# Modulation units placed anew in the weight ring, last-group sums taken product by product, zero products removed, and four waits moved, in a fused two-block transformer kernel

## The chip, the cores and the metric

The kernel runs as one program on one core of a Trainium2 chip, in float32. The metric is the device time of one execution in microseconds (us). Three executions of the kernel before took 1017.73, 1017.79 and 1018.97 us (median 1017.79). A fourth, recorded by the hardware profiler, took 1019.06 us; its trace spans 1017.3 us from the first to the last instruction, and all trace times below count from the start of that span.

## The reference, cut to what matters

A sequence of 256 tokens of width 1024 goes through two blocks. The first has two layers (`x + rms_norm(mixer(rms_norm(x)))`, four mixers of four heads each). The second, on which most of the change lies, has two layers whose inputs and residuals are modulated by a vector `c`:

```python
c_act = jax.nn.silu(c)
for i in range(DEPTH):                       # 2
    mods = jnp.split(c_act @ w_ada[i] + b_ada[i], 6, axis=-1)
    sh1, sc1, g1, sh2, sc2, g2 = [m[:, None, :] for m in mods]
    u = x * (1.0 + sc1) + sh1
    y = gla_mixer(...) if i == 0 else chunk_attention(...)
    x = layer_norm_2(DEEPNORM_ALPHA * x + (1.0 + g1) * y, ...)
    u = x * (1.0 + sc2) + sh2
    y = jnp.square(jax.nn.relu(u @ w1)) @ w2  # d_ff = 4096
    x = layer_norm_2(DEEPNORM_ALPHA * x + (1.0 + g2) * y, ...)
```

## The kernel before

**Names.** The 256 tokens are two tiles `t` of 128. `xt` is the residual stream, `xs` its normed form, `hT` the transposed, modulated input of the products (eight chunks of 128 features). `bank` is PSUM: eight banks of 128x512, `G[0..3]` and `A[0..3]`.

**The ring.** All large weights come as 180 units of 1 MB through six slots of `raw`. Unit `n` goes to slot `n % 6`. SyncE (SP) issues the transfers in order (L450), each after `used` of the same slot, that is, after the last reader of unit `n - 6`. A late reader of one unit therefore holds back that slot and all units after it in the queue. Most units are read by TensorE (PE). The modulation weights `w_ada` are units too, but VectorE (DVE) reads them: 24 units of the second layer's modulation go through `ada_unit_1`, by rows (`row_unit`, L905 and L909) or by columns (`column_unit`, L922). Their places in the ring are the table `ADA_1`, and the place in DVE's own program is where `ada_unit_1(ADA_1[a], a)` stands.

**GLA (N_GLA = unit 60 on).** Sixteen weight units and nine modulation units, `mma` six times, then `mmmm`, then `aaa`: eight of the nine are read during the mixer, the ninth (unit 84) in the first group of the feed-forward. `mixer_unit` and `mixer_sums` compute the projections with seven products in place of eight (a Strassen-like scheme whose sums DVE forms). Near the end, PE computes the last two gate projections into `G[2]` and `G[3]`, transposes the normed heads into `G[q]` for q = 0 to 3 (waiting for both gates before q = 2, L2413), and DVE multiplies by the gates (L1712). `out_product` and `out_sum`/`mixer_block` make the output projection.

**Feed-forward (`net` on PE, `groups` on DVE, `relu_groups` on ScalarE, ACT).** Sixteen groups of 256 hidden features. Group g has an up unit and a down unit; in layer 0 a modulation unit follows each of groups 1 to 15. For the first fifteen groups the down products also use seven products (`seven_products`, L2189) that accumulate over the groups in seven PSUM banks `SB`; before group 0 PE clears them by products on `zeros` (L2275). After the last of them DVE forms the four output blocks from the seven banks (`seven_sums`, L1529 to L1541) and adds the gated residual by column halves (`half_residual`, L1549 and L1552). The sixteenth group (`last_group`, L2241 and L2253) is computed plainly; its second half waits until DVE has read bank `A[2]` (`bank_free`), and its down products wait for `seven_ready`. Then come `modulation(1)` (L2132), `boundary` (L1326 to L1360) and the transposes of the next stage (L2141), copied to `hT` by ACT (L640).

**GpSimd (POOL)** forms the sums for three attention units in `quad_weights` (L523 to L528), the first of them as soon as the feed-forward's last unit is used. **The layer boundary in block one**: ACT squares the output halves (`y_square`, L611 to L616), then copies the transposed tile into `hT` (`layer_input`, L625), on which the first products of the next layer (L1921) wait.

The line that binds the ring to its readers:

```python
for s in range(SLOTS):
    sp.wait_ge(used[s], i)
    sp.dma_start(raw[:, s, :], units[i * SLOTS + s, :, :]).then_inc(landed[s], 16)
```

Of the kernel before, what the change touches and what calls it, by code (L numbers as in the profile page):

```python
# [14 lines left out]
P = 128  # L15
S = 256
# [60 lines left out]
AG = 9  # L77
NG = 16 + AG
N_GLA = DEPTH * U1
N_FF0 = N_GLA + NG  # L80
N_ATT = N_FF0 + 2 * GROUPS + 15
N_FF1 = N_ATT + 16

# [7 lines left out]
ADA_1 = [N_GLA + n for n in GA_AT] + [N_FF0 + 3 + 3 * g for g in range(SEVEN - 1)] + [N_FF0 + 2 + 3 * (SEVEN - 1)]  # L91
# [34 lines left out]
def build(nc, x, units, cols, small, post_g, consts, onehot, rel_bias, ccol, crow_in, colb_in, ada_rows,  # L126
          ln_rows, low_in, gk_in, att_line, v_row, out):
    with ExitStack() as ctx:  # L128
# [71 lines left out]
        def views(offset=0):  # L200
# [167 lines left out]
        tsum_ready, usum_ready = event("tsum_ready", 1), event("usum_ready", SEVEN - 1)  # L368
        last_up, bank_free = event("last_up", 1), event("bank_free", 1)
# [42 lines left out]
            ("ow_ready", 8), ("oi_ready", 2), ("op_ready", 7), ("ob_ready", 4)))  # L412

# [43 lines left out]
        def _(pool):  # L457
# [110 lines left out]
            n = N_FF1 + 2 * GROUPS - 1  # L568
# [6 lines left out]
        def _(act):  # L575
# [30 lines left out]
            def y_square(l, t):  # L606

                for i in range(2):
                    k = 2 * t + i
                    act.wait_ge(ob_ready.sem, ob_ready.at(l, k + 1))  # L610
                    act.activation(nl[:, 0:512], out_block[k], ACT.Square, accum_out=ssy[:, k:k + 1]).then_inc(osq_ready.sem, 1)  # L611
                    act.wait_ge(osq_ready.sem, osq_ready.at(l, k + 1))
                    if i == 0:
                        ch.do(act.activation(ybias[:, t:t + 1], ssy[:, k:k + 1], ACT.Identity, scale=1.0 / D, bias=eps_x[:]))
                ch.sync()
                act.activation(root[:, t:t + 1], ssy[:, k:k + 1], ACT.Sqrt, scale=1.0 / D,  # L616
                               bias=ybias[:, t:t + 1]).then_inc(sso_ready.sem, 1)

            def layer_input(l, t):

                for q in range(2 - t):
                    act.wait_ge(htp_ready.sem, htp_ready.at(l, 2 * t + q + 1))
                    for i in range(4):
                        c = 4 * q + i
                        act.activation(hT[:, c, t * P:(t + 1) * P], HB[t][q][:, i * P:(i + 1) * P], ACT.Copy,  # L625
                                       scale=pre[:, l, c:c + 1]).then_inc(ht_act.sem, 1)
# [20 lines left out]
            layer_input(0, 0)  # L647
            for l in range(DEPTH):

                layer_input(l, 1)  # L650
# [92 lines left out]
                y_square(l, 0)  # L743
                if l < DEPTH - 1:
                    x_square(l + 1, 0)
                else:
                    input_tile(0, 0, UB[0])
                y_square(l, 1)
                if l < DEPTH - 1:
                    layer_input(l + 1, 0)  # L750
                    x_square(l + 1, 1)
# [7 lines left out]
            def relu_groups(n0, per):  # L759

                step, lay = per // 3, n0 == N_FF1
                wait_used(act, 0, n0)
                act.activation(relu[:].rearrange("p c s -> p (c s)"), A[3][:], ACT.Relu).then_inc(relu_ready.sem, 1)
                for g in range(1, SEVEN):
# [4 lines left out]
                    wait_used(act, 0, n0 + 1 + step * (g - 1))  # L769
                    act.activation(prod[:, 4:7].rearrange("p i n -> p (i n)"), A[0][:, 0:3 * P], ACT.Copy).then_inc(prod_ready.sem, 1)  # L770
                n = n0 + step * SEVEN
# [3 lines left out]
                wait_used(act, 0, n)  # L775
# [56 lines left out]
            relu_groups(N_FF0, 9)  # L832
# [36 lines left out]
            relu_groups(N_FF1, 6)  # L869
# [9 lines left out]
        def _(dve):  # L879
# [644 lines left out]
            def seven_sums(last):  # L1524
# [3 lines left out]
                wait_used(dve, 0, last)  # L1528
                ch.do(dve.tensor_copy(c[0][0], p[0]))  # L1529
                ch.sync()  # L1530
                ch.do(dve.tensor_tensor(c[0][1], c[0][0], p[5], ALU.add))
                ch.do(dve.tensor_tensor(c[0][0], c[0][0], p[1], ALU.add))
                ch.sync(1)
                dve.sem_inc(bank_free.sem, 1)
                ch.do(dve.tensor_tensor(c[1][0], c[0][1], p[6], ALU.add))
                ch.do(dve.tensor_tensor(c[0][1], c[0][1], p[4], ALU.add))
                ch.sync(1)
                ch.do(dve.tensor_tensor(c[1][1], c[1][0], p[4], ALU.add))
                ch.do(dve.tensor_tensor(c[1][0], c[1][0], p[3], ALU.subtract))
                ch.sync(2)  # L1540
                dve.tensor_tensor(c[0][1], c[0][1], p[2], ALU.add).then_inc(seven_ready.sem, 1)  # L1541

            def half_residual(s, h):

                lay, g = s // 2, s % 2
                c = slice(h * 512, (h + 1) * 512)
                dve.wait_ge(seven_ready.sem, seven_ready.at(lay, 1))
                for t in range(NT):
                    ch.do(dve.tensor_tensor(ytmp[:, t, c], ytmp[:, t, c], gate_row[:, GATE_ROW[lay, g], c], ALU.mult))  # L1549
# [140 lines left out]
            for a in (4, 5):  # L1690
                ada_unit_1(ADA_1[a], a)
# [1041 lines left out]
```

## Time and profile before

| what | value |
|---|---|
| median of three executions | 1017.79 us (1017.73 to 1018.97) |
| the profiled execution: device time / span | 1019.06 us / 1017.3 us |
| PE matmul busy | 988.4 us, 97% |
| DVE busy | 773.6 us, 76% |
| ACT, POOL busy | 207.0 us (20%), 83.0 us (8%) |
| mean granted TensorE clock | 0.992 |
| DMA | 205.58 MB, mean 202 GB/s |

PE is busy for 988.4 of 1017.3 us, so what can be had without fewer products is at most the difference, 28.9 us, which includes the start and the tail. A row of the timeline reads: start in us, duration in us, engine, line, operation, tiles written and read, shapes, count of merged instructions, and in brackets how long the engine was idle before and what ended that. Each float32 product is recorded as two MATMUL instructions. The waits view sums such idle times by line and by what ended them.

### The profile page before, as it was taken

How to read it: one execution, taken by the hardware profiler on the slowest of the kernel's cores; microseconds unless marked ns; L12 is line 12 of the kernel's file. 1: busy time of each engine (PE TensorE's matmuls, PEld its weight loads, DVE VectorE, ACT ScalarE, POOL GpSimd, SP SyncE). 2: the span in 40 equal slices, each digit the busy share in tenths (PEclk: the TensorE clock that was granted, in tenths of full speed). 3: DMA queues.
4: the chain of work that ended last, by engine and by line, in shares of the span. 5: the costliest groups of instructions: out<-in, count | busy, mean ns of one | idle time of the engine just before them, and what ended most of it. 6: DMA issues, size and time to landing. Idle time of an engine off the chain costs nothing. (4 is left out here: it accounts for less than half of the span.)

```text
span 1017.3 us, 14206 instructions
## 1 busy us (share of the span) xinstructions
PE 988.4 (97%) x5326; PEld 722.5 (71%) x5328; DVE 773.6 (76%) x1761; ACT 207.0 (20%) x504; POOL 83.0 (8%) x91
## 2 busy tenths in 40 slices
PE   8999999999999999999899999989999999999996
PEld 4858755858766899747577777658996677777763
DVE  2697687696686887798799888985874677766677
ACT  4134314124322221201000000022223110000001
POOL 1100000000000000000002000062850000000020
PEclk9999999999999999999899999999999999999999
DMA  9955553855455746270879777824454345555511
GB/s 353 353 216 191 210 180 126 350 193 216 182 195 206 265 167 249 98 300 17 315 267 360 278 263 253 289 84 166 146 167 145 124 154 177 207 171 180 181 49 42
DMA packets 29916, 205.58 MB, mean 202 GB/s; under 512 B 3630, under 2 KB 3795, under 8 KB 6172
## 3 DMA queue, kind: packets, MB, share of 16 engines
q1 hardware_dynamic: 27116, 191.60, 51.6%
q0 software_dynamic: 2736, 13.11, 3.5%
q8 instruction: 42, 0.69, 0.3%
q14 instruction: 22, 0.18, 0.1%
HBM read 203.64 MB, written 1.05 MB: 201 GB/s over the span
## 5 line engine op out<-in xcount | busy, mean ns | idle before, releaser
L1859 PE MATMUL bank<-hT,raw 128*128 128x256 f32 x736 | 162.5, 380 | 0.0
L1859 PEld LDWEIGHTS bank<-hT,raw 128*128 128x128 f32 x736 | 138.7, 190 | 20.4 <-issue 1.7
L2189 PE MATMUL bank<-yT,arena 128*128 128x512 f32 x224 | 100.9, 593 | 0.4 <-DVE yT L1522 0.4
L2189 PE MATMUL bank<-raw,arena 128*128 128x512 f32 x180 | 88.7, 604 | 4.9 <-DMA raw<-units_dram 4.9
L2189 PEld LDWEIGHTS bank<-yT,arena 128*128 128x128 f32 x224 | 42.4, 190 | 54.5 <-issue 51.2
L922 DVE CUSTOM_DVE_ANT_0 raw<-raw,crow 128x1024 f32<-128x1024 f32 x64 | 75.4, 1220 | 1.1 <-DVEq L119 1.1
L2213 PEld LDWEIGHTS bank<-hT,raw 128*128 128x128 f32 x416 | 50.5, 192 | 12.4 <-issue 12.4
L768 ACT ACTIVATE arena<-bank 128x512 f32<-128x512 f32 x28 | 16.7, 597 | 196.9 <-PE bank L2213 196.9
L2213 PE MATMUL bank<-hT,raw 128*128 128x128 f32 x416 | 50.6, 275 | 0.0
L955 DVE SCALAR_TENSOR_TENSOR arena<-arena 128x256 f32<-128x256 f32 x120 | 48.4, 480 | 0.1
L2189 PEld LDWEIGHTS bank<-raw,arena 128*128 128x128 f32 x180 | 30.6, 194 | 22.0 <-issue 16.8
L1485 DVE TENSOR_TENSOR arena<-arena 128x256 f32<-128x256 f32 x28 | 13.4, 480 | 39.5 <-ACT arena L768 39.5
L2213 PE MATMUL bank<-arena 128*128 128x128 f32 x336 | 42.2, 275 | 0.0
L2213 PE MATMUL bank<-arena,gateT 128*128 128x128 f32 x336 | 42.2, 275 | 0.0
L2165 PE MATMUL bank<-hT,raw 128*128 128x128 f32 x256 | 37.2, 282 | 3.6 <-ACT hT L640 3.6
L909 DVE SCALAR_TENSOR_TENSOR ada<-raw,cact,ada 128x1024 f32<-128x1024 f32 x28 | 36.6, 1307 | 5.3 <-DMA raw<-units_dram 4.5
L2213 PEld LDWEIGHTS bank<-arena,gateT 128*128 128x128 f32 x336 | 39.9, 192 | 0.3
L2213 PEld LDWEIGHTS bank<-arena,raw 128*128 128x128 f32 x224 | 29.9, 194 | 13.9 <-issue 13.9
L2213 PEld LDWEIGHTS bank<-arena 128*128 128x128 f32 x336 | 39.7, 192 | 0.0
L770 ACT ACTIVATE arena<-bank 128x384 f32<-128x384 f32 x28 | 13.8, 491 | 114.1 <-PE bank L2213 114.1
L2165 PEld LDWEIGHTS bank<-hT,raw 128*128 128x128 f32 x256 | 32.7, 191 | 5.8 <-issue 5.2
L1939 PE MATMUL bank<-arena 128*128 128x512 f32 x72 | 32.4, 592 | 0.0
(462 smaller groups left out, 1817.6 us busy)
## 6 DMA issues: line engine op xcount, KB each, us to landing
raw<-units_dram SPq DMA_DIRECT2D x180, 1024.0 KB, 4.9
arena<-ln_rows_dram POOLq DMA_DIRECT2D x4, 1024.0 KB, 5.0
arena<-att_line_dram POOLq DMA_DIRECT2D x4, 512.0 KB, 5.5
arena<-small_dram POOLq DMA_DIRECT2D x2, 896.0 KB, 9.7
arena<-ada_rows_dram POOLq DMA_DIRECT2D x1, 1536.0 KB, 7.2
xt<-x_dram SPq DMA_DIRECT2D x2, 512.0 KB, 4.4
arena<-post_g_dram POOLq DMA_DIRECT2D x2, 512.0 KB, 8.7
kst<-consts_dram SPq DMA_DIRECT2D x1, 608.0 KB, 14.1
```

Of the source, the lines that this page charges most:

```text
L768: act.activation(prod[:, 0:4].rearrange("p i n -> p (i n)"), A[0][:], ACT.Copy).then_inc(prod_ready.sem, 1)
L770: act.activation(prod[:, 4:7].rearrange("p i n -> p (i n)"), A[0][:, 0:3 * P], ACT.Copy).then_inc(prod_ready.sem, 1)
L909: ins = dve.scalar_tensor_tensor(dst, w, cc, dst, ALU.mult, ALU.add)
L922: ins = dve.tensor_tensor_reduce(out=w, in0=w, in1=crow[:], scale=1.0, scalar=0.0, op0=ALU.mult, op1=ALU.add, accum_out=dst[:, c:c + 1])
L955: ins = dve.scalar_tensor_tensor(cacc[:, c, :], xg[:, c, j:j + S], w, cacc[:, c, :], ALU.mult, ALU.add)
L1485: ch.do(dve.tensor_tensor(csum[:, 0:5:4], prod[:, 0:1].to_broadcast([P, 2, P]), prod[:, 1:3], ALU.add))
L1859: mm = pe.matmul(b[:, c * S:(c + 1) * S], raw[:, s, k * 256 + c * P:k * 256 + (c + 1) * P], act_t[:, k, :], start=(k == 0), stop=(k == KC ...
L1939: mm = pe.matmul(OUT_BANKS[l][j][:], x[c] if isinstance(x, list) else x[:, c], y[c] if isinstance(y, list) else y[:, 512 * c:512 * (c + 1) ...
L2165: mm = pe.matmul(b[:, c * S + t * P:c * S + (t + 1) * P], raw[:, n % SLOTS, k * 256 + c * P:k * 256 + (c + 1) * P], hT[:, k, t * P:(t + 1) ...
L2189: return pe.matmul(SB[i][:], x, y, start=False, stop=stop)
L2213: mm = pe.matmul(A[0][:, i * P:(i + 1) * P], x(k), y(k), start=k == 0, stop=k == 3)
```

## The change

1. **Modulation units.** Two tables of letters set the ring: `GLA_ORDER` = `mma` four times, `mmaaaa`, `mmmmmmaaa` (eleven modulation units) and `FF_ORDER`, in which layer 0 has thirteen. On DVE unit a = 0 is read before the first stage's input, one more between the last mixer sums, three (a = 8, 9, 10) before the output sums, and groups 0 to 12 read one each; `coefficients(2)` and `(3)` follow group 12's.
2. **`seven_sums`.** The last group's seven products signal one by one (`last_product`), `5` is made before `4` and `6`, and DVE adds each bank when its product is done. The residual is now taken by tiles (`tile_residual`) and stands before the square that it followed.
3. **No zeros.** The first products carry `start=True`.
4. **Waits.** ACT at the layer boundary copies three chunks of `hT` before the last square; PE makes the first two products of mixer unit 0 before the decay rows and so before their wait; PE's transposes q = 2, 3 go to `A[2]`, `G[2]`, q = 3 waits for gate three only, and DVE waits for gate four; POOL starts `quad_weights` after both tiles are normed and its second one after `quad_tsum`.

```diff
-GW_AT = [w + w // 2 for w in range(12)] + [18 + w for w in range(4)]
-GA_AT = [3 * a + 2 for a in range(6)] + [22 + a for a in range(AG - 6)]
+GLA_ORDER = 4 * "mma" + "mmaaaa" + "mmmmmmaaa"
+FF_ORDER = ("u" + 13 * "uda" + "ud" + "dud", "u" + 14 * "ud" + "dud")
...
+        TURN_BANKS = (G[0], G[1], A[2], G[2])
...
-            wait_used(pool, 0, N_ATT - 1)
+            pool.wait_ge(xn_ready.sem, xn_ready.at(1, 2))
             quad_weights(0)
+            pool.wait_ge(quad_tsum, 1)
             quad_weights(1)
-            pool.wait_ge(xn_ready.sem, xn_ready.at(1, 2))
             quad_weights(2)
...
+                    y_square(l, 1, 0)
+                    layer_input(l + 1, 0, 0, 3)
+                    y_square(l, 1, 1)
+                    layer_input(l + 1, 0, 3, KC)
...
+                way = c[1][0]
+                dve.wait_ge(last_product.sem, last_product.at(lay, 1))
+                ch.do(dve.tensor_copy(way, p[0]))
+                ch.sync()
+                dve.wait_ge(last_product.sem, last_product.at(lay, 2))
+                ch.do(dve.tensor_tensor(c[0][0], way, p[1], ALU.add))
+                dve.wait_ge(last_product.sem, last_product.at(lay, 4))
+                dve.tensor_tensor(way, way, p[5], ALU.add).then_inc(bank_free.sem, 1)
+                dve.wait_ge(bank_free.sem, bank_free.at(lay, 1))
+                dve.wait_ge(last_product.sem, last_product.at(lay, 5))
+                ch.do(dve.tensor_tensor(c[0][1], way, p[4], ALU.add))
...
+                dve.tensor_tensor(c[1][0], way, p[3], ALU.subtract).then_inc(seven_ready.sem, 1)
...
                 for c in range(2):
+                    tile_residual(lay, c)
                     dve.wait_ge(relu_ready.sem, relu_ready.at(lay, 2 + c))
                     dve.tensor_tensor(hid[:, k, c], relu[:, c], relu[:, c], ALU.mult).then_inc(hid_ready.sem, 1)
-                    half_residual(s, c)
...
             for q in range(4):
+                if q == 2:
+                    out_weights(MIXER, 1, 1)
+                    out_weights(MIXER, 1, 2)
+                    dve.wait_ge(gate_ready, 4)
                 dve.wait_ge(ogp_ready, q + 1)
...
-            out_weights(MIXER, 1, 1)
-            out_weights(MIXER, 1, 2)
-            for a in (6, 7):
+            for a in (8, 9, 10):
                 ada_unit_1(ADA_1[a], a)
...
                 def product(i, x, y):
-                    return pe.matmul(SB[i][:], x, y, start=False, stop=stop)
+                    mm = pe.matmul(SB[i][:], x, y, start=g == 0, stop=stop)
+                    if stop and i != 3:
+                        mm.then_inc(last_product.sem, 1)
+                    return mm
...
-                    pe.matmul(b[:], zeros[:, 0:P], zeros[:], start=True, stop=False)
...
-            mixer_unit(0)
+            mixer_unit(0, between=decay_rows)
...
-                if q == 2:
-                    pe.wait_ge(gate_ready, 4)
+                if q == 3:
+                    pe.wait_ge(gate_ready, 3)
```

How the instructions stand on DVE between the gated heads and the output sums of the mixer, before (`raw,crow` and `raw,cact` mark modulation units, `arena<-raw` the weight sums of the output projection, `COPY arena<-bank` the first output sum):

```order
L1712 SCALAR_TENSOR_TENSOR yT<-bank,colb,gateT 128x256 x4
L1077 TENSOR_TENSOR arena<-yT 128x256
...
L1067 TENSOR_TENSOR arena<-raw,arena 128x1024
L1069 TENSOR_TENSOR arena<-arena,raw 128x1024
L1071 TENSOR_TENSOR arena<-raw 128x1024
L922 ISA raw,acc<-raw,crow 128x1024
L922 ISA acc 128x1
...
L1088 COPY arena<-bank 128x512
```

and now:

```order
L1087 TENSOR_TENSOR arena<-raw,arena 128x1024
L1089 TENSOR_TENSOR arena<-arena,raw 128x1024
L1091 TENSOR_TENSOR arena<-raw 128x1024
L1741 SCALAR_TENSOR_TENSOR yT<-bank,colb,gateT 128x256 x4
L1097 TENSOR_TENSOR arena<-yT 128x256
...
L925 TENSOR_SCALAR ada<-raw,cact 128x1024
L929 SCALAR_TENSOR_TENSOR ada<-raw,cact,ada 128x1024 x5
L1108 COPY arena<-bank 128x512
```

The three weight sums went ahead of the second gated pair, and three row units (six instructions) stand where two column units stood.

DVE at the end of layer 0's feed-forward, before:

```order
L1522 TENSOR_TENSOR gateT<-gateT,raw 128x512
L909 SCALAR_TENSOR_TENSOR ada<-raw,cact,ada 128x1024 x4
L1002 TENSOR_TENSOR arena<-acc,colb 128x16
...
L1529 COPY arena<-bank 128x512
...
L1541 TENSOR_TENSOR arena<-arena,bank 128x512
L1587 TENSOR_TENSOR arena<-arena 128x256
L1549 TENSOR_TENSOR arena<-arena 128x512 x2
L1552 SCALAR_TENSOR_TENSOR xt<-xt,arena 128x512 x2
```

and now:

```order
L1542 TENSOR_TENSOR gateT<-gateT,raw 128x512
L1551 COPY arena<-bank 128x512
L1554 TENSOR_TENSOR arena<-arena,bank 128x512
...
L1568 TENSOR_TENSOR arena<-arena,bank 128x512
L1576 TENSOR_TENSOR arena<-arena 128x512 x2
L1579 SCALAR_TENSOR_TENSOR xt<-xt,arena 128x512 x2
L1612 TENSOR_TENSOR arena<-arena 128x256
```

Two modulation units and the coefficients no longer stand ahead of the sums (they are in group 12 and before), and the first square (L1612, was L1587) follows its tile's residual.

## Rows read from the trace of the kernel before

**Rows 1.** Waits of PE: idle us in total, times, longest

```profile
PE bank L2189 <- DMA raw<-units_dram: 4.9, 1, 4.9
PE bank L2413 <- ACT gateT L816: 0.8, 1, 0.8
PE bank L2338 <- ACT arena L783: 0.5, 1, 0.5
```

**Rows 2.** Timeline of PE, feed-forward of layer 0, starts of groups 1 to 3

```profile
480.48 1.95 PE L2213 MATMUL bank<-hT,raw 128*128 128x128 f32 x16
...
489.11 3.78 PE L2189 MATMUL bank<-raw,arena 128*128 128x512 f32 x4 [4.88 <-DMA raw<-units_dram]
...
500.00 1.95 PE L2213 MATMUL bank<-hT,raw 128*128 128x128 f32 x16
...
512.27 1.95 PE L2213 MATMUL bank<-hT,raw 128*128 128x128 f32 x16
```

**Rows 3.** Timeline of DVE and of SP's queue at the same stall

```profile
482.76 4.00 DVE L909 SCALAR_TENSOR_TENSOR ada<-raw,cact,ada 128x1024 f32<-128x1024 f32 x3
...
484.22 1.96 SPq L450 DMA_DIRECT2D raw<-units_dram  x4
```

**Rows 4.** Windows: length, busy PE, PEld, DVE, ACT, POOL, PEclk, DMA share, GB/s

```profile
480.00:484.00 4.00, 4.00 (x34) 3.71 (x32) 3.93 (x6) 0.00 (x0) 0.00 (x0) 1.00 0.02 4
...
488.00:492.00 4.00, 2.89 (x4) 1.34 (x5) 2.59 (x4) 0.00 (x0) 0.00 (x0) 0.50 1.01 426
...
166.00:167.00 1.00, 1.00 (x3) 0.67 (x2) 1.00 (x1) 1.00 (x5) 0.00 (x0) 0.50 0.00 0
```

**Rows 5.** Timeline of all engines, layer boundary of block one

```profile
164.04 0.64 ACT L611 ACTIVATE arena<-gateT 128x512 f32<-128x512 f32 x1 [1.90 <-DVE gateT L1096]
...
165.00 2.16 ACT L625 ACTIVATE hT<-bank,pre 128x128 f32<-128x128 f32 x8
...
165.49 6.66 PE L1921 MATMUL bank<-raw,hT 128*128 128x352 f32 x16 [1.53 <-ACT hT L625]
...
169.65 0.75 DVE L1035 TENSOR_SCALAR xs<-xt,rst 128x1024 f32<-128x1024 f32 x1
...
171.99 1.04 PE L1909 MATMUL bank<-kst,xs 128*128 128x128 f32 x8
...
173.14 4.97 PE L1921 MATMUL bank<-raw,hT 128*128 128x352 f32 x16
```

**Rows 6.** Timeline of DVE and PE, starts of the two feed-forwards

```profile
468.37 0.69 DVE L1466 TENSOR_TENSOR arena<-hT,arena 128x512 f32<-128x512 f32 x1
...
469.79 1.95 PE L2213 MATMUL bank<-arena,gateT 128*128 128x128 f32 x16
...
814.80 0.69 DVE L1466 TENSOR_TENSOR arena<-hT,arena 128x512 f32<-128x512 f32 x1
...
815.79 1.24 PE L2275 MATMUL bank<-zeros 128*128 128x512 bf16 x5
```

**Rows 7.** Timeline of DVE and PE, end of the feed-forward of layer 0

```profile
648.76 5.31 DVE L909 SCALAR_TENSOR_TENSOR ada<-raw,cact,ada 128x1024 f32<-128x1024 f32 x4
...
653.28 3.62 PE L2241 MATMUL bank<-hT,raw 128*128 128x256 f32 x16
...
655.75 0.69 DVE L1529 COPY arena<-bank 128x512 f32<-128x512 f32 x1 [0.24 <-DVE arena L1016]
...
664.01 5.42 PE L2253 MATMUL bank<-raw,arena 128*128 128x512 f32 x12 [0.82 <-DVE arena L1587]
...
666.40 1.29 DVE L1326 TENSOR_TENSOR arena<-bank,arena 128x512 f32<-128x512 f32 x2
...
673.84 1.09 PE L2141 MATMUL bank<-kst,xs 128*128 128x128 f32 x8 [0.98 <-DVE xs L1360]
```

**Rows 8.** Line L1360, six tiles: ns min/median/max, first and last start us

```profile
L1360 DVE TENSOR_SCALAR xs<-xt,bag,rst x6: 811/814/1891, 453.2 to 808.2; 128x1024 f32<-128x1024 f32 x6
```

**Rows 9.** Timeline of DVE, first sum of the last boundary

```profile
1004.85 0.69 DVE L1387 CUSTOM_DVE_ANT_0 xt<-bank,xt 128x512 f32<-128x512 f32 x1 [0.21 <-DVEq L119]
```

More of the change, by code:

```diff
@@ L74, with places @@
 ARENA = 21104
-AG = 9
-NG = 16 + AG
+SEVEN = GROUPS - 1
+GLA_ORDER = 4 * "mma" + "mmaaaa" + "mmmmmmaaa"
+FF_ORDER = ("u" + 13 * "uda" + "ud" + "dud", "u" + 14 * "ud" + "dud")
 N_GLA = DEPTH * U1
-N_FF0 = N_GLA + NG
-N_ATT = N_FF0 + 2 * GROUPS + 15
+N_FF0 = N_GLA + len(GLA_ORDER)
+N_ATT = N_FF0 + len(FF_ORDER[0])
 N_FF1 = N_ATT + 16
-SEVEN = GROUPS - 1
-GW_AT = [w + w // 2 for w in range(12)] + [18 + w for w in range(4)]
-GA_AT = [3 * a + 2 for a in range(6)] + [22 + a for a in range(AG - 6)]
-ADA_1 = [N_GLA + n for n in GA_AT] + [N_FF0 + 3 + 3 * g for g in range(SEVEN - 1)] + [N_FF0 + 2 + 3 * (SEVEN - 1)]
+def places(order, what, at=0):
+    return [at + n for n, c in enumerate(order) if c == what]
+UP, DOWN = ([places(FF_ORDER[lay], c, (N_FF0, N_FF1)[lay]) for lay in range(2)] for c in "ud")
+assert all(len(n) == GROUPS for n in UP + DOWN)
+GW_AT, GA_AT = places(GLA_ORDER, "m"), places(GLA_ORDER, "a")
+AG = len(GA_AT)
+ADA_1 = [N_GLA + n for n in GA_AT] + places(FF_ORDER[0], "a", N_FF0)
+assert len(GW_AT) == 16 and len(ADA_1) == 24
 RE = 2 * DEPTH
@@ L628, in root_of, with layer_input @@
+            def layer_input(l, t, c0, c1):
+                for c in range(c0, c1):
+                    q, i = c // 4, c % 4
+                    if i == 0:
+                        act.wait_ge(htp_ready.sem, htp_ready.at(l, 2 * t + q + 1))
+                    act.activation(hT[:, c, t * P:(t + 1) * P], HB[t][q][:, i * P:(i + 1) * P], ACT.Copy,
+                                   scale=pre[:, l, c:c + 1]).then_inc(ht_act.sem, 1)
             def root_of(s, t):
@@ L831, in _ @@
             stage_tiles(1)
-            relu_groups(N_FF0, 9)
+            relu_groups(0)
             stage_tiles(2)
@@ L1550, in half_residual @@
-                for t in range(NT):
+                for c in h:
+                    ch.do(dve.tensor_tensor(ytmp[:, t, c], ytmp[:, t, c], gate_row[:, GATE_ROW[lay, 1], c], ALU.mult))
+                for c in h:
                     ch.sync(1)
@@ L1553, in half_residual, with groups @@
                 ch.sync()
-            def groups(s, n0, per):
-                step, lay = per // 3, s // 2
+            def groups(s):
+                lay = s // 2
+                up, down = UP[lay], DOWN[lay]
                 token_sums(s, tsum, tsum_ready.sem)
@@ L1562, in groups @@
                     up_half_sums(s, g + 1)
-                    weight_sums(n0 + 2 + step * g)
+                    weight_sums(down[g])
                     up_rest_sums(s, g + 1)
@@ L1757, in _ @@
             normed(0, 1)
-            up_sums(N_FF0 + 1, 1)
+            up_sums(UP[0][1], 1)
             stage_tiles(1)
-            groups(1, N_FF0, 9)
-            boundary(1, y_told(1, 3) + y_used(N_ATT - 1))
+            groups(1)
+            boundary(1, y_told(1, 3) + y_used(DOWN[0][-1]))
             stage_tiles(2)
@@ L2305, in mixer_unit @@
                 product(0, lambda k: w[:, k, 0:P], lambda k: hT[:, k, 0:P])
+                if between is not None:
+                    between()
                 product(1, lambda k: w[:, 4 + k, 0:P], lambda k: hT[:, 4 + k, 0:P])
@@ L2687, in lay_out @@
         f2 = [w2[256 * g:256 * (g + 1)].reshape(2, P, D).transpose(1, 0, 2).reshape(P, UNIT) for g in range(GROUPS)]
-        units.append(f1[0])
-        for g in range(1, SEVEN):
-            units += [f1[g], f2[g - 1]]
-            if l == 0:
-                units.append(ada1[AG + g - 1])
-        units.append(f2[SEVEN - 1])
-        if l == 0:
-            units.append(ada1[AG + SEVEN - 1])
-        units += [f1[SEVEN], f2[SEVEN]]
+        rest = {"u": iter(f1), "d": iter(f2), "a": iter(ada1[AG:])}
+        units += [next(rest[c]) for c in FF_ORDER[l]]
         if l == 0:
```

179 lines of the change are left out of this document (79 added, 100 removed).

## The prediction, made before the changed kernel was run

> **What bounds the kernel now.** The table above says it first: PE is busy for 97% of the span, at almost full clock. So the question is never "which engine is shorter" but "where does PE stand still, where does it run at half clock, and which of its products go". I read four views in that order. The waits view of PE gives the stops by cause: the longest single one is 4.9 us for a weight unit, and two short ones of 0.8 and 0.5 us end on ACT [rows 1]. The timeline round the long stop shows what it really costs [rows 2], and the queue's own timeline what released it [rows 3]. The windows tell a full DMA system from an empty one, and half clock from full [rows 4]. Last come the timelines at the places where one stage hands over to the next [rows 5 to 8]; the reader is to look there for the time in brackets and its releaser.
>
> **The ring, 7.2 us.** A group takes 500.00 to 512.27, that is 12.27 us; the group from 480.48 took until 500.00, 19.52 us [rows 2]. The difference, 7.25 us, is the 4.88 us stop plus some 2.4 us of slow products behind it: four of them took 3.78 us [rows 2], at a granted clock of 0.50, the 1.2 GHz level [rows 4]. Why did the unit come late? In the four microseconds before the stop the DMA share was 0.02 [rows 4]: nothing was being fetched. SP issued at 484.22, within DVE's modulation products of group 0, and the unit landed 4.9 us later, when PE went on [rows 2, 3]. Counting units: the down unit of group 1 is unit 90, slot 0, whose predecessor is unit 84, the ninth modulation unit, which DVE reads only in group 0. It held up slot 0 and all behind it. In the new order N_FF0 is 87, that down unit is 92, and its predecessor 86 is read by DVE before the mixer's output sums, a stage earlier. Every other predecessor of group 0's and 1's units (81 to 85) is read earlier still. In the groups each slot is released in the group before its unit is needed, as before, and the group at 500.00 shows no stop. I take the whole 7.25 us. Bounds: 0 if another unit takes its place, 7.25 if none does.
>
> DVE pays for this. Before the output sums it now does three row units, six instructions, where two column units stood; a row instruction takes about 1.3 us (5.31 for four [rows 7]), so 2.4 to 2.9 us more. But it no longer stands still for the last two output units: they come in slots 82 % 6 and 83 % 6, whose predecessors are modulation units 76 and 77, read before the gates are computed; before, the last one's was the last gate's weight unit. Two more units stand in idle time of DVE in the mixer. Behind the three units the output sums are queued, and PE's feed-forward behind these. I cost it at nothing; without the cover it would be 2.9 us.
>
> **Two waits in the mixer, 1.2 us.** The decay rows' wait on ACT (0.5) goes behind two products that need nothing, and the wait for gate four (0.8) leaves PE [rows 1]; DVE takes it, but reaches it only after three weight sums. PE stays the bound up to the feed-forward, so I take 0.5 + 0.8, less 0.1. Bounds 0 and 1.3.
>
> **The layer boundary, 1.2 us.** PE waited 1.53 us for ACT's first copy at 165.00; ACT had idled 1.90 us before the last square at 164.04 [rows 5]. Now three copies (0.27 each, 2.16 for eight) use that idle time. PE starts almost 1.5 us sooner and ACT's next five copies follow in time. But PE then meets the second tile: its normed form was ready at 169.65 + 0.75 = 170.40, and this chain hangs on the last square, which the three copies push back by about 0.3 (0 to 0.8). So PE can begin the second transposes at 170.8 instead of 171.99 [rows 5]: a gain of 1.2, not 1.5. The rest becomes a new wait of up to 1.8 us on DVE's `xs`. Whether the first tile runs at half clock, as it did (6.66 us against 4.97 for the same products, clock 0.50 [rows 4, 5]), no longer matters, since PE would wait anyway. Bounds 0.7 and 1.5.
>
> **No zeros, 2.3 us.** Seven products on zeros per feed-forward; five are recorded in 1.24 us, the last one's tail lying over the next product, so about 0.22 each, 1.5 per feed-forward [rows 6]. In layer 1 the token sums end at 814.80 + 0.69 = 815.49, about when PE gets there: all 1.5 is gained. In layer 0 they end at 469.06 and PE went on at 469.79 [rows 6], so the first six give about 0.65 and then a wait for DVE; with the seventh, 0.85. Bounds 1.5 and 3.
>
> **The end of the first feed-forward, 2.6 us.** Before, DVE did 5.31 us of modulation and the coefficients, and began the seven sums at 655.75, 2.5 us after PE's last product of seven (653.28) [rows 7]. Now it starts at about 649 and follows: PE makes a 128x512 product of two instructions in some 0.9 us (5.42 for twelve), DVE needs 0.69 or less per sum (0.65 per operation in a pair of 1.29) [rows 7], and after PE's last at 653.28 only three sums remain, so `seven_ready` comes near 655.1. A tile's residual is four of these operations, 2.6 us: first square near 658.2, second near 661.3. PE meanwhile runs without a stop: the last group's up products 7.2 us (3.62 for half of them [rows 7]), the last group's down products (sixteen instructions) and the modulation rows (eight) another 10.3 at 0.43 each, the tail of the twelve taken off: from 653.28 to 670.8. The stops of 0.82 and 0.98 us [rows 7] and the shorter ones between go. Does DVE have the tile by then? It began the boundary at 666.40 [rows 7]; now it waits for PE's second output block (four products of 0.86 after 660.5), near 663.9, and is there for the next step about 2.9 us earlier, so the tile, ready for PE at 673.84, is ready at 670.9 even at the old durations. PE begins the transposes at 670.8 to 670.9 in place of 673.84: 3.0 us. Against it: group 12 now carries both a row unit and the coefficients (654.07 to 655.75, 1.7 us [rows 7]), of which DVE's idle time in a group takes the larger part. Between 0 and 1.7 I take 0.5 us of PE waiting, since two places in each group let DVE wait for ACT. Net 2.6 us, bounds 1 and 3.4.
>
> The slowest L1360 took 1891 ns against 811 [rows 8]; it is this boundary's first tile, while POOL was forming `quad_weights`. The Trainium skill (SBUF — State Buffer, Who interferes with whom) says that the two engines share a port pair as an exclusive lock, the loser blocked for the whole instruction; the trace agrees in size. By that rule the moved POOL wait gives DVE 1.1 us back on this chain. In my sum it is worth at most 0.1, because PE's own work until 670.8 then covers it. POOL's second and third unit now come after the token sums, but PE needs them only in the second and third quarter of the first heads, behind three projections: no cost.
>
> **The end of the kernel, 0.4 us.** DVE began the last boundary at 1004.85, just free of the residual (0.21 us idle for its own work) [rows 9]. Freed of it sooner, it is bound by PE's output blocks, whose last ends no earlier than before, counted from PE's last product of seven. Between nothing and one more operation of 0.7 us on each side, I take 0.4, bounds 0 and 1.4.
>
> **The sum.** 7.25 + 1.2 + 1.2 + 2.3 + 2.6 + 0.4 = 14.95 us. The profiled execution took 1019.06 us (span 1017.3), so 1004.1 and a span of 1002.3. That execution lies 1.3 us above the median of the three others, 1017.79; against the median it is 1002.8. I give **1003.0**.
>
> **The rivals.**
> - *The clock falls in a new place.* Before the half-clock stretch at 166 PE had stopped for 1.53 us [rows 4, 5]; my new wait at about 169 to 170.8 is as long, and stands before products that nothing hides. The price is what the same products lost there, 6.66 - 4.97 = 1.7 us: 1004.7. Chance 0.2. The Trainium skill (TensorE: Matmul & The Clock Gate, What's actually happening) says that activity, not demand, releases the throttle; by that rule any new stop is suspect, and so would be the zero products' removal in layer 0, where PE now idles 0.65 us.
> - *The stop moves rather than goes.* DVE is now the only reader ahead of units 90 to 92, and any one read late stops PE in group 0 or 1. For it: slots are few, and DVE is nearly full in groups 1 to 4. Against: by the count above these three are released before the output sums. A stop of the old size costs 7.25: 1010.2. Chance 0.1. That the change does not do what it says (the unit late for bandwidth, not for its slot) is the same case; the DMA share of 0.02 ahead of the stop speaks against it [rows 4], though it was 1.01 once the four issues had gone.
> - *The sums do not pay.* DVE meets PE's products too late, or group 12 falls further behind, and 2.6 becomes 0: 1005.6. Chance 0.08.
> - *Slower.* Unit 86 is issued only when PE starts on the output projection's second half-input, and DVE's output sums, `xs`, the first feed-forward and thus PE are queued behind its reading. From the time at which it is just hidden, each us that it lands later costs one. By my count it is just in time; to be slower than 1017.8 it would have to land over 15 us later than the 4.9 us seen at the stop. Price 15 and more: 1018 or above, chance 0.02.
>
> **How the numbers follow.** Forecast 0.60, clock 0.20, moved stop 0.10, sums 0.08, slower 0.02. A measurement of this kernel tells about 0.2% from no change, 2 us. The forecast's own bounds (mixer and zeros a little less, boundary a little more) are about 999.8 to 1005; with the clock and the sums the range reaches 1007.5, and leaves out most of the moved stop and the slower case. All cases but the last are faster by more than 2 us: faster 0.97, same 0.01, slower 0.02.
>
> **What would show it.** In the new profile: no wait of PE on a DMA in the feed-forward, and groups 0 to 3 all of 12.3 us; no row of `zeros` after the start, and a wait of PE on DVE's token sums in layer 0 only; a wait on `xs` of up to 1.8 us at the layer boundary with none on the first copy; the seven sums starting before PE's last product; no PE wait on POOL or on `asum`. The forecast is wrong if PE busy plus PE's stops does not fall by about 14 us, and wrong in its largest term if a DMA stop stands anywhere between the mixer and group 3.

## The result, and the profile after

The changed kernel took 1004.47 us in the median of four runs (1003.33 to 1005.85), the kernel before 1018.38 us beside it (1017.73 to 1019.66). The ratio is 0.9862, with a 95% interval of 0.9845 to 0.9880: 1.4% faster. The forecast was 1003.0 us, its range 999.8 to 1007.5. The profiled execution took 1004.16 us (span 1002.4), 14.90 us less than the profiled one of before; the forecast's sum was 14.95. The medians lie 13.91 us apart.

PE's waits after the change (idle us in total, times, longest); the three rows of [rows 1] are gone, and the two longest that remain hang on DVE and ACT:

```profile
PE bank L2192 <- ACT hT L657: 3.6, 8, 1.3
PE bank L1936 <- DVE xs L1055: 2.7, 3, 1.7
PE bank L1928 <- POOL zeros L474: 1.3, 1, 1.3
PE bank L1948 <- ACT hT L642: 1.1, 1, 1.1
PE bank L2243 <- DVE arena L1486: 0.5, 1, 0.5
PE bank L2216 <- DVE yT L1542: 0.4, 1, 0.4
```

The starts of groups 1 to 3, on PE's timeline, answer to [rows 2], and the windows over the same stretch (busy PE, PEld, DVE, ACT, POOL, then PEclk, DMA share, GB/s) to [rows 4]:

```profile
477.56 1.95 PE L2243 MATMUL bank<-hT,raw 128*128 128x128 f32 x16
...
489.83 1.95 PE L2243 MATMUL bank<-hT,raw 128*128 128x128 f32 x16
...
502.10 1.95 PE L2243 MATMUL bank<-hT,raw 128*128 128x128 f32 x16
```

```profile
480.00:484.00 4.00, 4.00 (x27) 3.04 (x26) 3.58 (x7) 0.60 (x1) 0.00 (x0) 1.00 0.75 260
484.00:488.00 4.00, 4.00 (x22) 2.68 (x21) 3.02 (x8) 0.49 (x1) 0.00 (x0) 1.00 0.74 258
488.00:492.00 4.00, 4.00 (x25) 2.93 (x24) 3.93 (x9) 0.00 (x0) 0.00 (x0) 1.00 0.65 240
```

Group 1 takes 12.27 us where it took 19.52. The DMA share is even, where it had been 0.02 and then 1.01, and the clock stays at 1.00.

The layer boundary, which answers to [rows 5]: no wait for the first copy, three copies, the square, five copies, and the new wait on `xs`:

```profile
163.93 0.89 ACT L642 ACTIVATE hT<-bank,pre 128x128 f32<-128x128 f32 x3 [1.42 <-PE bank L1936]
...
164.44 4.97 PE L1948 MATMUL bank<-raw,hT 128*128 128x352 f32 x16
164.70 0.64 ACT L626 ACTIVATE arena<-gateT 128x512 f32<-128x512 f32 x1
...
165.66 1.38 ACT L642 ACTIVATE hT<-bank,pre 128x128 f32<-128x128 f32 x5
...
171.11 1.09 PE L1936 MATMUL bank<-kst,xs 128*128 128x128 f32 x8 [1.70 <-DVE xs L1055]
```

The end of the first feed-forward, which answers to [rows 7]: DVE takes up the sums while PE still makes the last group's products, waits for some of them, and has the first tile's `xs` before PE needs it:

```profile
639.00 0.68 DVE L1551 COPY arena<-bank 128x512 f32<-128x512 f32 x1
...
641.26 0.69 DVE L1556 TENSOR_TENSOR arena<-arena,bank 128x512 f32<-128x512 f32 x1 [0.85 <-PE bank L2216]
...
645.02 0.69 DVE L1568 TENSOR_TENSOR arena<-arena,bank 128x512 f32<-128x512 f32 x1
...
653.38 0.69 DVE L1346 TENSOR_TENSOR arena<-bank,arena 128x512 f32<-128x512 f32 x1 [1.73 <-PE bank L2283]
...
659.07 0.81 DVE L1380 TENSOR_SCALAR xs<-xt,bag,rst 128x1024 f32<-128x1024 f32 x1
...
660.84 1.04 PE L2168 MATMUL bank<-kst,xs 128*128 128x128 f32 x8
```

Laid over one another, the two PE timelines give the place of every microsecond (before to after, start of the same products):

| stretch | forecast | measured |
|---|---|---|
| start of the kernel (another DVE and ACT wait there) | 0 | -0.38 |
| layer boundary | 1.2 | 1.20 |
| two waits in the mixer (0.34 and 0.97) | 1.2 | 1.31 |
| zeros, layer 0 and layer 1 | 0.85 + 1.5 | 0.78 + 1.43 |
| the ring, group 1 | 7.25 | 7.25 |
| lost again in the groups (0.40 of it in group 12) | -0.5 | -0.52 |
| end of the first feed-forward, gross | 3.0 | 3.35 |
| end of the kernel | 0.4 | 0.41 |

With 0.07 us of small shifts this is 14.90 us. Every term that was forecast came out within 0.35 us, and yet the experiments show that two of them had another cause than the one given.

### The profile page after: what moved, and what is told of

The parts are those of the page before. It is cut to its first block, busy times and chain, and to the rows that moved or that the text cites. A ratio compares the mean times of both kernels' runs of the same rounds, so it can differ in the third digit from the quotient of the medians.

```text
span 1002.4 us, 14184 instructions
## 1 busy us (share of the span) xinstructions
PE 982.2 (98%) x5314; PEld 719.6 (72%) x5314; DVE 771.3 (77%) x1761; ACT 206.7 (21%) x504; POOL 82.8 (8%) x91
## 4 chain that ended last, share of the span: by engine, by line
PE 50%; DVE 3%; issue 0%; ACT 0%; DVEq 0%; ACTq 0%
PE bank L2216 17%; PE bank L2243 16%; PE bank L2500 6%; PE bank L2519 2%; PE bank L2192 2%; PE bank L2271 1%; PE bank L2283 1%; PE bank L1896 1%; PE bank L2485 1%; PE bank L1886 1%; PE bank L1913 1%; PE bank L2539 0%; PE bank L2159 0%; PE bank L2530 0%; PE bank L2528 0%
```

## The experiments

"Longer" and "shorter" below are read like the table, by laying PE's timeline over that of the changed kernel's profile. That resolves about 0.05 us, where the medians of the runs resolve 1 to 2 us.

**e1: the old ring with all the rest of the change.**

```diff
-GLA_ORDER = 4 * "mma" + "mmaaaa" + "mmmmmmaaa"
-FF_ORDER = ("u" + 13 * "uda" + "ud" + "dud", "u" + 14 * "ud" + "dud")
+GLA_ORDER = 6 * "mma" + "mmmmaaa"
+FF_ORDER = ("u" + 14 * "uda" + "daud", "u" + 14 * "ud" + "dud")
```

and DVE's reads at their old places (unit 84 in group 0, the last unit and the coefficients behind the groups).

> The changed kernel with the old order of units in the ring and the old places of the modulation reads on DVE; all else of the change stays. Slot theory: unit 84 is again read only in group 0, so PE stops for about 4.9 us on a weight unit ahead of group 1's products and runs some of them at clock 0.50; the group from about 477.6 takes 19.5 us instead of 12.3, and the run about 7.25 us longer than the changed kernel, near 1011.7. The coefficients are again behind the groups, so the end of the first feed-forward gives back up to 2 us more: up to 1013.5. Rival (what helped was that PE's or DVE's other edits loosened the fetching): no stop of over 1 us in the feed-forward, about 1004.5.

Measured: 1018.62 us, ratio to before 0.9989 (0.9975 to 1.0003). The whole gain is gone, 13.84 us in the timelines. PE's waits and timeline of this kernel:

```profile
PE bank L2217 <- DMA raw<-units_dram: 4.8, 1, 4.8
...
PE bank L2284 <- DVE arena L1615: 2.9, 1, 2.9
...
PE bank L2272 <- DVE arena L1556: 0.9, 1, 0.9
PE bank L1967 <- DVE yT L1742: 0.8, 1, 0.8
```

```profile
487.15 3.78 PE L2217 MATMUL bank<-raw,arena 128*128 128x512 f32 x4 [4.80 <-DMA raw<-units_dram]
...
656.15 3.72 PE L2272 MATMUL bank<-hT,raw 128*128 128x256 f32 x16 [0.91 <-DVE arena L1556]
...
662.78 8.64 PE L2284 MATMUL bank<-raw,arena 128*128 128x512 f32 x16 [2.91 <-DVE arena L1615]
```

The slot theory stands: the stop and the slow products are back, 19.61 us for the group instead of 12.27. What was missed is the rest. In the mixer DVE again stands 5.31 us for an output unit ahead of the gate turns (4.98 in the kernel before), and PE, which no longer waits for gate four and so comes sooner, waits 0.83 us for the first of these turns: most of the 0.97 us won at that wait is lost again. And at the end of the feed-forward 5.85 us are lost where I allowed 2: with the last unit and the coefficients behind the groups DVE begins the sums at 654.08, and PE runs into `bank_free` (0.91), into the last squares, which now stand behind a whole tile's residual (2.91), and into half clock (8.64 us for sixteen products that took 7.03). The new order of sums and residual is good only while DVE is early: over the same stretch the kernel before, whose DVE is as late but whose sums and residual are the old ones, takes 3.35 us more than the changed kernel, and so 2.5 us less than this one; 1.6 us of the 2.5 are the half clock.

**e2: the kernel before with one read moved.**

```diff
-                        if g == 0:
-                            ada_unit_1(ADA_1[8], 8)
...
-            for a in (6, 7):
+            for a in (6, 7, 8):
```

> The kernel before with one line moved: DVE reads the ninth modulation unit (unit 84) ahead of the output sums instead of in group 0; the order of the ring stays. Slot theory: the stop of 4.9 us and the slow products behind it go, 7.25 us less, about 1011; DVE's extra 2.6 us ahead of the output sums may show as up to 1 us of waiting. Rival (the place in the ring is what counts, since unit 84 would land too late to be read early, or its successors would): a stop of 2 us or more stands at the output sums or in group 0, and the gain is under 4 us, 1014 or more.

Measured: 1015.31 us, ratio to before 0.9958 (0.9942 to 0.9975). No stop on a DMA stands in the feed-forward, and from the first group to the last products of seven this kernel gains 7.16 us on the one before. The profile as a whole gains only 5.41, because 0.85 us are lost at the start, 0.78 by DVE's extra unit (PE waits 0.94 us on `xs` ahead of the feed-forward) and 1.63 by half clock at 344 (the last section), while 1.54 are won at the layer boundary (see e4). So the reading of one unit was the whole stall; its place in the ring was not.

```profile
464.38 1.09 PE L2139 MATMUL bank<-kst,xs 128*128 128x128 f32 x8 [0.94 <-DVE xs L1360]
```

**e3: the old sums and residual in the changed kernel.** `seven_sums` waits for all seven products and then works in pairs; the residual goes by column halves behind each square.

```diff
-                dve.wait_ge(last_product.sem, last_product.at(lay, 1))
+                wait_used(dve, 0, last)
...
-                    tile_residual(lay, c)
                     dve.wait_ge(relu_ready.sem, relu_ready.at(lay, 2 + c))
                     dve.tensor_tensor(hid[:, k, c], relu[:, c], relu[:, c], ALU.mult).then_inc(hid_ready.sem, 1)
+                    half_residual(s, c)
```

> The changed kernel with the seven sums begun only after all seven products of the last group (in two pairs, and with the residual in halves by column), as before the change; ring, zeros and waits stay changed. If following the products one by one is what pays: PE's stops of 0.8 and 1 us at the end of the first feed-forward return, and the kernel is 1.0 to 1.5 us longer there and 0.4 us longer at its end, about 1006. Rival (the gain came from moving the last modulation unit and the coefficients away, and PE's work covers the sums anyway): under 0.3 us at the first feed-forward, 1004.8.

Measured: 1005.16 us, 0.9854 (0.9837 to 0.9870). At the end of the first feed-forward nothing is lost: PE starts the boundary's transposes at 660.73, as in the changed kernel (660.84), and without a wait, though DVE begins the sums 4.7 us later:

```profile
643.73 0.69 DVE L1550 COPY arena<-bank 128x512 f32<-128x512 f32 x1 [4.84 <-PE bank L2210]
...
654.37 1.29 DVE L1346 TENSOR_TENSOR arena<-bank,arena 128x512 f32<-128x512 f32 x2
```

At the end of the kernel the old sums and residual cost 0.40 us. (The profile also has a stop of 1.93 us at 964, which is not theirs; see e8.) The rival of the expectation is right: at the first feed-forward the following of single products pays nothing. What is left there is DVE's freed time; no run takes back the last modulation unit and the coefficients alone (e1 does it together with the whole ring).

**e4: all eight copies behind both squares again.**

```diff
-                    layer_input(l + 1, 0, 0, 3)
                     y_square(l, 1, 1)
-                    layer_input(l + 1, 0, 3, KC)
+                    layer_input(l + 1, 0, 0, KC)
```

> The changed kernel with ACT's order at the layer boundary as before: the eight copies of the first tile behind both squares. Forecast's step: PE waits about 1.5 us for the first copy again, the wait on DVE's xs shrinks to almost nothing, and the boundary ends 1.2 us later: 1005.6. On the clock: if the stop of 1.5 us right behind the one of about 0.5 us is what lowered it in the kernel before, the granted clock falls to 0.50 for about 3.4 us near 166 again; if it was chance, it stays at 1.00 and the boundary still ends about 1 us later, because DVE's chain to xs sets it.

Measured: 1004.82 us, 0.9855 (0.9836 to 0.9875); in the timelines 1.19 us longer at the boundary, with the clock at half again. That looks like a proof of my step, but e2 has the same old order, and there the clock did not fall. PE's rows at the boundary, first of e4, then of e2:

```profile
165.28 6.66 PE L1947 MATMUL bank<-raw,hT 128*128 128x352 f32 x16 [1.53 <-ACT hT L642]
171.78 1.04 PE L1935 MATMUL bank<-kst,xs 128*128 128x128 f32 x8
```

```profile
166.33 4.97 PE L1919 MATMUL bank<-raw,hT 128*128 128x352 f32 x16 [1.53 <-ACT hT L625]
171.30 1.09 PE L1907 MATMUL bank<-kst,xs 128*128 128x128 f32 x8
```

From the first tile's transposes to the second's: 9.13 us before, 9.11 in e4, 7.59 in e2, 7.87 in the changed kernel. At full clock the old order is thus 0.28 us quicker than the new one; the new one is 1.2 us quicker where the first tile's products fall to half clock. What the copies bring is room in which such a fall is hidden.

**e5: the zeros again.** Both feed-forwards open their seven banks by products on zeros, and all products add.

> The changed kernel with the seven products on zeros ahead of both feed-forwards again (all products then add). Forecast's step: 0.8 us longer at the first feed-forward, where the wait of 0.45 us for DVE's token sums goes, and 1.5 us at the second: 2.3 us in all, about 1006.7. Rival (the zeros were partly hidden in the second too): 1.5 us or less in all.

Measured: 1007.08 us, 0.9881 (0.9861 to 0.9901). In the timelines 0.75 us longer in layer 0 and 1.43 in layer 1, as forecast. The profile is 3.68 us longer in all: the other 1.5 us is lost at the start, where PE's products at 10.61 us ran at half clock and took 6.69 us, in place of 5.34 in the changed kernel.

**e6: POOL's first weights for the second attention at their old place**, during the boundary of the first feed-forward.

```diff
-            pool.wait_ge(xn_ready.sem, xn_ready.at(1, 2))
+            wait_used(pool, 0, N_ATT - 1)
             quad_weights(0)
-            pool.wait_ge(quad_tsum, 1)
             quad_weights(1)
+            pool.wait_ge(xn_ready.sem, xn_ready.at(1, 2))
```

> The changed kernel with POOL's weights for the second attention formed at the old place, during the boundary of the first feed-forward. The old slow DVE instruction (1.9 us in place of 0.8) comes back for the first tile of that boundary. Forecast: PE's own products cover it, at most 0.1 us. Rival (DVE's chain is by now the bound there, so that the port contention shows in full): 1.1 us, about 1005.6, with a stop of PE on xs of about 1 us near 661.

Measured: 1006.18 us, 0.9880 (0.9859 to 0.9901). The port does what it did: `xs` takes 1.63 us beside POOL in place of 0.81. PE does not notice; the shift against the changed kernel is 2.14 us both in the groups and after this boundary.

```profile
661.03 1.26 POOL L538 TENSOR_TENSOR arena<-raw 128x512 f32<-128x512 f32 x1
661.21 1.63 DVE L1379 TENSOR_SCALAR xs<-xt,bag,rst 128x1024 f32<-128x1024 f32 x1
...
662.98 1.04 PE L2167 MATMUL bank<-kst,xs 128*128 128x128 f32 x8
```

The 2.14 us arise ahead of the edit: 0.45 at the start, and 1.69 at the layer boundary, where the same instructions as in the changed kernel met half clock. The window has PEclk in the third column from the end:

```profile
171.57 1.09 PE L1935 MATMUL bank<-kst,xs 128*128 128x128 f32 x8 [1.70 <-DVE xs L1054]
172.77 6.67 PE L1947 MATMUL bank<-raw,hT 128*128 128x352 f32 x16
```

```profile
174.00:176.00 2.00, 2.00 (x4) 1.02 (x4) 2.00 (x3) 0.70 (x1) 0.00 (x0) 0.50 0.00 0
```

**e7: both mixer waits at their old places**, and with gate four's wait DVE's two weight sums behind the turns.

> The changed kernel with the decay rows' products and the wait for gate four at their old places (and the old banks of the gate transposes). Forecast's step: the two stops of PE, 0.5 and 0.8 us, come back, 1.2 us in all, 1005.7. Rival: DVE's own lateness in the mixer makes one of them worthless, 0.5 us or less.

Measured: 1006.75 us, 0.9881 (0.9864 to 0.9899). The stops come back, 0.34 us and 0.97 us, as in the table. But another 1.31 us is lost ahead of the feed-forward, which neither theory had:

```profile
463.38 0.87 PE L2166 MATMUL bank<-kst,xs 128*128 128x128 f32 x6 [1.48 <-DVE xs L1380]
```

**e10: only the two weight sums back behind the turns**, gate four's wait left on DVE, to find the cause of that.

```diff
                 if q == 2:
-                    out_weights(MIXER, 1, 1)
-                    out_weights(MIXER, 1, 2)
                     dve.wait_ge(gate_ready, 4)
...
+            out_weights(MIXER, 1, 1)
+            out_weights(MIXER, 1, 2)
             for a in (8, 9, 10):
```

> The changed kernel with DVE's last two weight sums of the output projection again behind the gate turns, and gate four's wait still on DVE. Theory from e7: their place ahead of the turns is what hides the three modulation units, and without it DVE comes to the boundary's xs about 1.3 us late; 1.3 us longer. Rival: in e7 it was the wait on PE that made DVE late, and here nothing is lost (under 0.3 us).

Measured: 1006.44 us, 0.9874 (0.9858 to 0.9891). PE again waits 1.49 us on `xs`, and 1.32 us are lost: the whole of e7's surplus. The weight sums ahead of the turns are a cover for DVE's three modulation units; e2, which has them behind the turns, showed the price of one unit more, 0.78.

**e8: two edits on top of the change.** Two copies instead of three ahead of the square, and the coefficients in group 13.

```diff
-                    layer_input(l + 1, 0, 0, 3)
+                    layer_input(l + 1, 0, 0, 2)
                     y_square(l, 1, 1)
-                    layer_input(l + 1, 0, 3, KC)
+                    layer_input(l + 1, 0, 2, KC)
...
-                        if AG + g == len(ADA_1) - 1:
-                            coefficients(2)
-                            coefficients(3)
+                    if lay == 0 and AG + g == len(ADA_1):
+                        coefficients(2)
+                        coefficients(3)
```

> The changed kernel with two further edits: two of the eight copies ahead of ACT's last square at the layer boundary in place of three, and the coefficients (1.7 us of DVE) in group 13, which has no modulation unit, in place of group 12. The square then starts when its input is there (about 0.3 us sooner), and PE's wait on xs ends 0.3 us sooner; PE's 0.4 us lost in groups 12 and 13 is won back. 0.7 us less than the changed kernel, 1003.8 (span 1001.7). If the coefficients were not what made PE wait in group 12, 0.3 us less.

Measured: 1005.07 us, 0.9859 (0.9838 to 0.9880), no gain to be seen. Up to 960 the timeline is 0.47 us shorter, start aside: 0.26 at the layer boundary, and 0.40 in group 12, of which PE gives back 0.19 at the next boundary. (Two copies also undo the 0.28 us of e4: 7.61 us from tile to tile.) Then 3.1 us are lost in group 14 of the last feed-forward:

```profile
960.37 5.10 POOL L587 TENSOR_TENSOR raw<-raw,arena 128x1024 f32<-128x1024 f32 x2 [95.41 <-DMA raw<-units_dram]
960.41 2.84 DVE L1499 TENSOR_TENSOR arena<-raw,arena 128x512 f32<-128x512 f32 x1
963.40 3.34 PE L2243 MATMUL bank<-arena 128*128 128x128 f32 x16 [1.92 <-DVE arena L1499]
```

The last weight unit lands, and POOL starts to multiply it by the gate 0.04 us ahead of the DVE operation for which PE waits. That operation takes 2.84 us in place of 0.69. In the changed kernel's own profile DVE was first, by 0.19 us:

```profile
961.15 0.69 DVE L1499 TENSOR_TENSOR arena<-raw,arena 128x512 f32<-128x512 f32 x1
961.34 5.03 POOL L587 TENSOR_TENSOR raw<-raw,arena 128x1024 f32<-128x1024 f32 x2 [95.66 <-DMA raw<-units_dram]
```

By the Trainium skill (SBUF — State Buffer, Who interferes with whom) a DVE instruction with two inputs in SBUF contends with a GpSimd instruction that reads SBUF, the port pair that they share is an exclusive lock, and the order of issue decides who blocks. The trace agrees: POOL's first instruction took 2.34 us, and DVE, which came second, lost 2.15 and ended 0.55 us after it. The collision stands in e3, e8 and e10, three of the nine profiles of kernels with the new ring that leave POOL free here (the changed kernel's two are among the nine), with stops of 1.9 us, of which 1.4 to 1.5 remain in PE's timeline of e3 and e10; e8 had half clock behind it too, which the other two had not. The three kernels with the old ring start the same two instructions as close together (DVE 0.12 us ahead in the kernel before), so the danger is not new.

**e9: e8 with a guard.**

```diff
             wait_landed(pool, 0, n)
+            pool.wait_ge(usum_ready.sem, usum_ready.at(1, SEVEN - 1))
```

> The kernel of e8 (two copies ahead of the square, coefficients in group 13) with one more wait on POOL: its two products on the last weight unit begin only when DVE has formed the up sums of the last group. Theory: in e8 and e3 POOL began 0.04 us ahead of that DVE operation, which then took 2.84 us in place of 0.69 and stopped PE for 1.9 us. With the wait no such stop is seen in any profile, and from the start of the two kernels' products the run is 0.47 us shorter than the changed kernel, about 1004 or a little less. Rival (the stop comes from the unit landing late, not from POOL): the stop of 1.9 us on DVE's up sums stands again.

Measured: 1003.64 us (1003.27 to 1004.36 in five runs), 0.9842 (0.9829 to 0.9856). No such stop in the profile, e8's gain of 0.48 us kept up to group 14, and 0.30 of it lost there (PE waits 0.73 us on DVE's `yT` in place of 0.42, since POOL's second product still meets a DVE operation). Its median is the lowest of all; net of the start, its timeline is 0.18 us shorter than the changed kernel's.

**e11: the changed kernel once more**, on the chip of e9.

> The changed kernel itself once more, beside e9 on the same chip. 1004.5 within 1 us. On the clock: the places where it falls to 0.50 for some 3.4 us are expected to differ from the first profile (none, until the end) in about one profile of three.

Measured: 1005.39 us (1003.27 to 1006.16), 0.9855 (0.9841 to 0.9868). Its profile repeats the first one within 0.15 us everywhere, and the clock does not fall before the kernel's end. e9's median is 1.75 us lower, but the fastest runs are equal (1003.27 both) and the intervals of the two ratios overlap, so what is sure of e9 is small: 0.18 us in the timelines, and no collision in its one profile, where the guard puts POOL behind DVE.

## Why the prediction was right, and where its reasons were not

**The ring** was right in place, cause and size (7.25 forecast and measured; e2 has 7.16 from one read alone, e1 brings it back). That DVE's three units cost nothing was right too: DVE waited 0.87 us for unit 86, and began the output sums at 441.14, 2.66 us earlier than before (1.17 of it is the shift of the whole by then), since its wait for an output unit had gone. But I had named the gone wait as the whole cover, and the weight sums placed ahead of the turns are a part of it: with the wait gone and only these back behind the turns, 1.3 us shows (e10). The price without any cover, put at 2.9, was not measured.

**The mixer** gave 1.31 for 1.2. **The zeros** gave 0.78 and 1.43 for 0.85 and 1.5, with the 0.45 us wait on the token sums that was said (0.65).

**The layer boundary** gave the 1.2 us, and the wait of 1.70 on `xs` (up to 1.8). The step that failed is "a gain of 1.2, not 1.5" as a gain of ACT's order: I compared with a first tile at half clock and took that as a fixed cost of the old order. It is not; e2 has it at full clock, and there the new order is 0.28 us behind, which is the square that I said would be pushed back by about 0.3. That the profiles show 1.20 is thus luck: the one profile of the kernel before had the fall and the changed kernel's had none.

**The end of the first feed-forward** gave 3.35 gross and 0.52 lost again, 2.83 for 2.6 (3.0 less 0.5 is 2.5; the sum had 2.6). The gross gain was larger because PE's own work from its last product of seven to the transposes took 17.21 us and not 17.5. Group 12's loss was expected at 0.5 and is 0.40; e8 shows that the coefficients cause it, for it goes with them. The step that failed is the attribution: of my two reasons, DVE free of the last unit and the coefficients, and DVE following the products, the second gives 0.0 (e3), because PE has 17 us of work of its own to cover it; what remains is the first, which no run took back by itself. My rival "the sums do not pay" had tied the whole 2.6 us to them and was wrong in that.

**The end of the kernel** gave 0.41 for 0.4, and this one does come from the new sums and residual (e3: 0.40).

**The port**: worth at most 0.1 us at the first boundary, by my sum; e6 shows 0.0. I had looked for it in one place only. It matters in another, at the last weight unit, and there DVE was ahead by 0.19 us in the changed kernel's first profile and by 0.01 in its second (e11). The collision, which was in no term and no rival, costs 1.4 us or more.

**The rivals.** The clock did fall behind the new stop of 1.70 us, with the forecast price (6.67 in place of 4.97, 1.7 us), but in e6 and not in the changed kernel's own two profiles, though the instructions up to there are the same. It was a matter of executions, not of a kernel. The moved stop and the late unit did not come. That the change could fail as a whole by its parts' dependence, as e1 does, was not among the rivals.

**The number.** The profiles are 14.90 us apart where the sum had 14.95, but the median of the changed kernel, 1004.47, lies 1.5 us above the 1003.0. Of this 0.6 is the kernel before, whose median of four is 1018.38 where three runs had given 1017.79. The rest is the gain between the medians, 13.91 us. The 14.95 had been worked out from the profiled execution of the kernel before, 1019.06 us and slower than the three others, and was taken off their median. Why the medians lie 1 us less apart than the profiles is not shown; 1 us is also as fine as they resolve.

## What to carry to other kernels

Before costing a reordering, ask of each part what it needs from the others: at the end of the first feed-forward the new sums were worth nothing with DVE early and about minus 2.5 us with DVE late, depending on reads moved elsewhere. Do not take a stretch at half clock as part of a program's price without a second execution. Where two engines that share a port both run freely, order them by a wait when one of them feeds the engine that bounds.

## What the hardware showed that I had not expected

**Half clock comes and goes between executions.** The thirteen profiles (before, after, e1 to e11) have nine falls to 0.50 ahead of the kernels' ends. At the layer boundary with the old order (a stop of 1.53 us, 0.5 us of stops shortly before) it fell in two of three; with the new order, behind a stop of 1.70 us (1.24 in e8 and e9), in one of ten. Behind the 1.9 us stops at group 14 it fell in one of three. At the long stops it fell each time (the unit's 4.9 and 4.8 us in the kernel before and e1, the 2.9 us in e1), and in e5 it fell once at the start. In e2 it fell at 344 behind a stop of 0.46 us only, which the kernel before and e7 have too, without a fall:

```profile
342.23 1.98 PE L2336 MATMUL bank<-wgk,arena 17*128 17x512 f32 x4 [0.46 <-ACT arena L783]
344.13 3.29 PE L2297 MATMUL bank<-hT,raw 128*128 128x128 f32 x16
```

Sixteen such products take 1.95 us elsewhere. A fall costs 1.5 to 1.7 us at the places where it can be read alone (e2, e6, the old order of the layer boundary). It is a part of the spread of the runs: of e11's five, the three with a mean granted clock of 0.997 took 1003.27 to 1005.39 us, the two with 0.995 took 1005.50 and 1006.16. What sets it off is open: the length of the stop ahead alone does not decide it, and no run here tried for its cause.

**A collision at a port is decided by hundredths of a microsecond.** DVE's operation took 0.69 us in all ten profiles in which it began ahead of POOL, the closest by 0.01 us (e11, below), and 2.83 to 2.85 in the three in which it began 0.04 to 0.06 us behind (e3, e8, e10).

```profile
961.25 0.69 DVE L1499 TENSOR_TENSOR arena<-raw,arena 128x512 f32<-128x512 f32 x1
961.26 5.21 POOL L587 TENSOR_TENSOR raw<-raw,arena 128x1024 f32<-128x1024 f32 x2 [95.48 <-DMA raw<-units_dram]
```
